# First norm's modulation rows: from split weights on four columns of the array to raw float32 weights on its four column strips

## The reference

```python
silu_c = jax.nn.silu(c)          # (1, 2048)
silu_cc = jax.nn.silu(c_ctx)     # (2048,)
mod = (silu_c @ w_ada[l] + b_ada[l])[:, None, :]       # w_ada[l]: 2048 x 12288
mod_c = silu_cc @ w_ada[l] + b_ada[l]
sh_a, sc_a, gt_a, sh_f, sc_f, gt_f = jnp.split(mod, 6, axis=-1)
h = rms_norm(x, g_attn[l]) * (1.0 + sc_a) + sh_a
hc = rms_norm(xc, g_attn[l]) * (1.0 + csc_a) + csh_a
# then h @ w_in, hc @ w_in (2048 x 4928), four attention mixers, w_out, ffn, second block
```

## Time and profile before

| | |
|---|---|
| median of three runs | 3089.66 us (3085.1 to 3093.73) |
| span of the profiled execution | 3084.6 us, mean granted clock 0.967 |
| PE / DVE / ACT / POOL busy | 2872.8 / 1828.0 / 1222.2 / 254.9 us |
| read from HBM | 572.42 MB, 187 GB/s over the span |
| head stage (before the first win matmul) | 0 to 195.55 us |

### The profile page before, as it was taken

One profiled execution on the slowest core, in us unless ns is written; L12 is line 12 of the kernel. 1 busy time (PEld: TensorE's weight loads), 2 busy tenths in 40 slices (PEclk: granted clock), 3 DMA queues, 4 the chain that ended last, 5 costly groups with the idle time before them and its releaser, 6 DMA issues.

```text
span 3084.6 us, 33987 instructions
## 1 busy us (share of the span) xinstructions
PE 2872.8 (93%) x12623; PEld 2288.0 (74%) x12623; DVE 1828.0 (59%) x2117; ACT 1222.2 (40%) x1561; POOL 254.9 (8%) x233
## 2 busy tenths in 40 slices
PE   3788998988989999999989998899999999999997
PEld 2257776756868888888867887788877888888886
DVE  2888988257655555555565444645455655665555
ACT  4542222234434444444434444444444444444443
POOL 3405233000010000000024000000000000000000
PEclk8899999978999999999999999999999999999998
DMA  8788988201755555555545553255545655555652
GB/s 210 253 268 291 310 292 299 97 14 56 254 179 191 191 185 196 190 191 190 190 142 187 195 196 111 95 193 194 195 162 171 201 182 191 188 191 184 197 190 95
DMA packets 284109, 578.93 MB, mean 188 GB/s; under 512 B 9885, under 2 KB 12610, under 8 KB 281466
## 3 DMA queue, kind: packets, MB, share of 16 engines
q1 hardware_dynamic: 280234, 557.00, 55.0%
q0 software_dynamic: 3792, 20.84, 2.1%
HBM read 572.42 MB, written 5.28 MB: 187 GB/s over the span
## 4 chain that ended last, share of the span: by engine, by line
issue 63%; PE 17%; DVE 12%; DVEq 2%; POOL 2%; ACT 1%; DMA 1%; POOLq 1%; ACTq 0%
DVE proj_ctx L1367 6%; PE bank L327 4%; PE bank L329 4%; PE bank L328 4%; DVE w_lo L323 3%; DVEq L1366 2%; PE bank L553 2%; PE bank L586 1%; ACT probs L660 1%; POOL na_rpb_T L1812 1%; PE bank L1649 1%; PE bank L1650 0%; PE bank L1678 0%; DMA w_raw<-in_w_ada 0%; PE bank L1659 0%
## 5 line engine op out<-in xcount | busy, mean ns | idle before, releaser
L323 DVE TENSOR_TENSOR w_lo<-w_raw,w_hi 128x1024 fp32r<-128x1024 f32 (+2 forms) x928 | 1136.5, 1247 | 748.4 <-ACT w_hi L315 735.9
L315 ACT ACTIVATE w_hi<-w_raw 128x1024 fp32r<-128x1024 f32 (+2 forms) x928 | 964.5, 1054 | 1370.9 <-PE bank L329 1118.8
L327 PE MATMUL bank<-w_hi,xa_hi 128*128 128x512 f32 (+1 forms) x2304 | 907.0, 394 | 35.8 <-DVE w_lo L323 32.9
L329 PE MATMUL bank<-w_hi,xa_lo 128*128 128x512 f32 (+1 forms) x2304 | 899.0, 390 | 0.0
L328 PE MATMUL bank<-w_lo,xa_hi 128*128 128x512 f32 (+1 forms) x2304 | 898.8, 390 | 0.0
L327 PEld LDWEIGHTS bank<-w_hi,xa_hi 128*128 128x128 f32 x2304 | 435.7, 189 | 144.1 <-DVE w_lo L323 32.8
L329 PEld LDWEIGHTS bank<-w_hi,xa_lo 128*128 128x128 f32 x2304 | 435.5, 189 | 90.7
L328 PEld LDWEIGHTS bank<-w_lo,xa_hi 128*128 128x128 f32 x2304 | 435.9, 189 | 87.5
L327 PE MATMUL bank<-w_hi,ffn_act_hi 128*128 128x512 f32 x864 | 338.9, 392 | 7.9 <-DVE w_lo L323 7.9
L328 PE MATMUL bank<-w_lo,ffn_act_hi 128*128 128x512 f32 x864 | 338.3, 392 | 0.0
L329 PE MATMUL bank<-w_hi,ffn_act_lo 128*128 128x512 f32 x864 | 338.0, 391 | 0.0
(11 more groups left out here) (274 smaller groups left out, 1870.0 us busy)
## 6 DMA issues: line engine op xcount, KB each, us to landing
w_raw<-in_w_in SPq DMA_DIRECT2D x116, 1024.0 KB, 5.1
w_raw<-in_w_ada SPq DMA_DIRECT2D x96, 1024.0 KB, 5.2
w_raw<-in_w_up SPq DMA_DIRECT2D x64, 1024.0 KB, 5.2
w_raw<-in_w_down SPq DMA_DIRECT2D x64, 1024.0 KB, 5.1
w_raw<-in_ffn_wg SPq DMA_DIRECT2D x44, 1024.0 KB, 5.2
w_raw<-in_ffn_wu SPq DMA_DIRECT2D x44, 1024.0 KB, 5.2
w_raw<-in_ffn_wd SPq DMA_DIRECT2D x44, 1024.0 KB, 5.1
w_raw<-in_w_out SPq DMA_DIRECT2D x32, 1024.0 KB, 5.1
```

What stands on the lines that cost most here:

```text
L315: act.activation(whi[:, slot, ks, 0:w], raw[:, q, ks, 0:w], ACT.Copy)\
L323: dve.tensor_tensor(wlo[:, slot, ks, 0:w], raw[:, q, ks, 0:w], whi[:, slot, ks, 0:w].bitcast(F32), ALU.subtract).then_inc(sem("lo_made"), 1)
L327: pe.matmul(out, xh, wh, start=first, stop=False)
L329: return pe.matmul(out, xl, wh, start=False, stop=last)
```

## The change

Head-stage units are no longer split. PE multiplies the raw float32 weights with plain float32 matmuls: slice j of a unit goes to partitions 32j to 32j+31 of the bank, with a stationary of 32 columns (16 copies of the silu value for x, 16 for the context). So the four slices of a unit lie on the four column strips of the array. DVE adds the whole bank and the bias, loaded to 32 partitions, in one instruction (`take_sums`); `spread_row` sums the strips with a 128-row stationary that picks one row of each strip. A slot is free again when PE has used it (`ada_used`). The table transfers move from POOL to the head of ACT's queue, the bands from chunk 0 to chunk 3, POOL's store of the bias behind all four `modulate`, and the turning of group 3 from before the first win unit to between the second and the third.

```diff
-U_MIX = 4 * N_ADA_1
+N_LOAD_1 = N_ADA_1
+U_MIX = 0
...
-            wait(sp, "lo_made", 8 * u4 + (2 * q - 6))
+            if isinstance(u4, int) and u4 <= 0:
+                wait(sp, "ada_used", 4 * (u4 + N_LOAD_1) + (q - 3))
+            else:
+                wait(sp, "lo_made", 8 * u4 + (2 * q - 6))
             sp.dma_start(raw[:, q, 0:k, 0:w], src).then_inc(sem(f"landed{q}"), 16)
...
-                sp.dma_start(rows_of(c % 2)[4:5, :], t["b_ada"][:, ada_cols(c)]).then_inc(sem(f"b_loaded{c % 2}"), 16)
+                wait(sp, "ada_rows", c - 1)
+                sp.dma_start(b_rows[0:32, c % 2, :], t["b_ada"][:, ada_cols(c)].to_broadcast([32, NCH]))\
+                    .then_inc(sem(f"b_loaded{c % 2}"), 16)
...
         def _(act):
 
+            with nc.allow_non_contiguous_dma(reason="31 x 28 table, once"):
+                act.wait_ge(sem("memsets"), 2)
+                for h in range(4):
+                    for p in (0, 32):
+                        act.dma_start(narpb[p:p + 31, h * 7:h * 7 + 7], t["na_rpb"][0, h, 4:11, :].rearrange("r m -> m r"))\
+                            .then_inc(sem("na_tables_loaded"), 16)
+            act.dma_start(band[:, :], t["na_band"]).then_inc(sem("na_tables_loaded"), 16)
+            act.dma_start(namask[:, :], t["na_mask"]).then_inc(sem("na_tables_loaded"), 16)
...
-            for c in range(N_ADA_1):
-                hi(act, c, 0)
-                hi(act, c, 1)
-                if c:
-                    copy_rows(c - 1, (c - 1) % 2, 4 * c, 2 + (c - 1) % 2)
-                hi(act, c, 2)
-                hi(act, c, 3)
...
+            for g in range(3):
+                turn_h_act(act, g)
...
+            for v in range(2):
+                m = dve.tensor_copy(c32[:, :, 16 * v:16 * v + 16],
+                                    ps[7][:, 16 * v:16 * v + 16].rearrange("p (k a) -> p k a", a=1)
+                                    .to_broadcast([P, 16, 16]))
...
+            def take_sums(c):
+
+                dve.wait_ge(sem("ada_used"), 4 * c + 4)
+                dve.wait_ge(sem(f"b_loaded{c % 2}"), 8 * (c - c % 2) + 16)
+                wait(dve, "ada_combined", c - 1)
+                dve.tensor_tensor(rows_1[:, c % 2, :], ps[2 + c % 2][:, :], b_rows[:, c % 2, :], ALU.add)\
+                    .then_inc(sem("ada_rows"), 1)
+
             for c in range(N_ADA_1):
-                lo(dve, c, 0)
-                lo(dve, c, 1)
-                lo(dve, c, 2)
                 if c:
                     take(c - 1)
-                lo(dve, c, 3)
+                take_sums(c)
...
+            take(N_ADA_1 - 1)
...
-                if i == 0:
-                    take(N_ADA_1 - 1)
+                if i == 1:
                     turn_h_dve(dve, 3)
...
-            def ada_unit(u4, q, k0, bank):
+            def ada_unit(c, q, bank):
+
+                pe.wait_ge(sem(f"landed{q}"), 16 * c + 16)
                 for j in range(KQ):
...
+                    m = pe.matmul(ps[bank][32 * j:32 * j + 32, :], c32[:, 4 * q + j, :], raw[:, q, j, :],
+                                  start=q == 0, stop=q == 3)
+                m.then_inc(sem("ada_used"), 1)
...
-                    m = pe.matmul(ps[v][:, :], spread[:, v, :], rows_of(c % 2), start=True, stop=True)
+                    m = pe.matmul(ps[spread_bank(c) + v][:, :], pick[:, v:v + 1].to_broadcast([P, P]),
+                                  rows_1[:, c % 2, :], start=True, stop=True)
...
-                if c == 0:
+                if c == 3:
...
             spread_row(N_ADA_1 - 1)
-            turn_h_pe(pe, 3)
-            pe.wait_ge(sem("h_lo"), 16)
...
+                if i == 2:
+                    turn_h_pe(pe, 3)
+                if i < 4:
+                    pe.wait_ge(sem("h_lo"), 4 * i + 4)
```

More of the change, by code:

```diff
@@ L286, in build, with spread_bank @@
         STEPS, STEPS2 = head_steps(), head_steps_2()
+        def spread_bank(c):
+            return 2 if c == N_ADA_1 - 1 else 0
         def load(sp, u4, q, src, k=KQ, w=NCH):
@@ L309, in hi @@
             slot = q % 2 if slot is None else slot
-            act.wait_ge(sem(f"landed{q}"), 16 * u4 + 16)
+            act.wait_ge(sem(f"landed{q}"), 16 * u4 + (16 * N_LOAD_1 + 16))
             for h in range(2):
@@ L1034, in b_piece @@
             def b_piece(c):
[L1036 to L1037 removed]
+                wait(sp, "ada_rows", c - 1)
+                sp.dma_start(b_rows[0:32, c % 2, :], t["b_ada"][:, ada_cols(c)].to_broadcast([32, NCH]))\
+                    .then_inc(sem(f"b_loaded{c % 2}"), 16)
+            sp.wait_ge(sem("memsets"), 4)
             for c in range(N_ADA_1):
                 for q in range(4):
[L1041 removed]
+                    load(sp, c - N_LOAD_1, q, w_ada_v[:, q, :, ada_cols(c)])
                 b_piece(c)
@@ L1117, in _ @@
             m.then_inc(sem("x_squares"), 1)
[L1119 to L1123, removed]
-            for c in range(N_ADA_1):
-                hi(act, c, 0)
-                hi(act, c, 1)
-                if c:
-                    copy_rows(c - 1, (c - 1) % 2, 4 * c, 2 + (c - 1) % 2)
-                hi(act, c, 2)
-                hi(act, c, 3)
-                if c == 0:
[L1133 to L1141, removed]
+            act.wait_ge(sem("na_tables_loaded"), 160)
+            act.activation(bandr[:, :], band[:, :], ACT.Copy)
+            act.activation(narpbr[:, :], narpb[:, :], ACT.Copy).then_inc(sem("na_rpb_hi"), 1)
+            act.wait_ge(sem("x_rstd"), 1)
+            for i in range(4):
+                m = act.activation(xin[:, i, :], xin[:, i, :], ACT.Copy, scale=stat(RSTD + i))
+            m.then_inc(sem("x_scaled"), 1)
+            for g in range(3):
+                turn_h_act(act, g)
             def win_copy(c):
@@ L1357, in multiply @@
                 acc = late_sums(c % 2)
-                dve.wait_ge(sem(f"landed{u % 4}"), 16 * (u // 4) + 16)
+                dve.wait_ge(sem(f"landed{u % 4}"), 16 * (u // 4 + N_LOAD_1) + 16)
                 if k == 0 and c >= N_ADA_1 + 2:
@@ L1805, in _ @@
             pool.dma_start(gvec[:, :], bcast(t["g_attn"], D)).then_inc(sem("g_attn_loaded"), 16)
-            with nc.allow_non_contiguous_dma(reason="31 x 28 table, once"):
-                pool.wait_ge(sem("memsets"), 2)
-                for h in range(4):
-                    for p in (0, 32):
-                        pool.dma_start(narpb[p:p + 31, h * 7:h * 7 + 7], t["na_rpb"][0, h, 4:11, :].rearrange("r m -> m r"))\
-                            .then_inc(sem("na_tables_loaded"), 16)
-            pool.dma_start(band[:, :], t["na_band"]).then_inc(sem("na_tables_loaded"), 16)
-            pool.dma_start(namask[:, :], t["na_mask"]).then_inc(sem("na_tables_loaded"), 16)
             rstd_pool(pool, "x", 4, "_squares")
@@ L1825, in _ @@
             pool.wait_ge(sem("x_scaled"), 1)
-            modulate(0)
+            for q in range(4):
+                modulate(q)
             pool.wait_ge(sem("na_bias_made"), 1)
             pool.dma_start(nab_d, nab_1[:, :, :, :]).then_inc(sem("na_bias_stored"), 16)
-            for q in range(1, 4):
-                modulate(q)
             def norm(x, g, width, n, col):
```

55 lines of the change are left out of this document (19 added, 36 removed).

## The result

| | before | changed |
|---|---|---|
| median | 3089.84 us (four runs) | 3044.06 us (3043.91 to 3046.9, four runs) |
| ratio | | 0.9852, 95% interval 0.984 to 0.9865 |
| span of the profiled execution | 3084.6 us | 3045.1 us |
| first transposition behind the mixer stage | 587.1 us | 547.3 us |

A forecast was written before the change was run, and what follows sets the result against it. Head bound by a 26 us load stall, then DVE's split; now load-bound: 60 + 72 + 4.5, `take(7)` at 144, third `w_lo` at 164.1 instead of 203.92. Span 3084.6 less 39, median 5.1 above: 3051 us, range 3032 to 3088.

The forecast's parts named there:

- The unit on PE (1.9 us): Head stage: a unit's eight matmul records on PE take 1.9 us, hidden behind a load of 3.0 us.
- all four strips together: PE's unit if all four column strips overlap: the time of two records, or 0.95 us.
- Rival 1: Strips do not overlap, so PE bounds the head at 3.45 to 3.7 us a unit: 3082 to 3090 us; chance 0.16.
- Rival 2: Each change of strip on PE exposes its weight load: a unit takes 6.2 us, 3127 us and up; chance 0.07.
- The first eight units (60 us): Head loads: the eighth unit lands at 60 us, slightly earlier than 60.8 because PE rather than DVE frees slots.
- The first chunks share the engines with the same transfers as before, whoever issues them: First head loads: moving the table transfers to another queue changes nothing, so the eighth unit lands at about 60 us.
- rival 3: Tables on ACT's queue land after 60 us, each us late costing one; 0.08 late but a gain, 0.03 beyond 100 us.
- The loads (72 + 4.5 us): Remaining 24 head units at 350 GB/s, 3.0 us each, 72 us, plus 4.5 for bias store and pieces: last lands at 136.5.
- 2 us at half clock: Cost of PE's bands in chunk 3 if the clock is half; at full clock the four slots in flight cover them.
- Behind the last unit: End of the head: PE's unit, `take_sums`, `spread_row`, `take(7)` and semaphore hops bring `take(7)`'s end to 144 us.
- The seam (20.1 us): Head to mixer stage: 20.1 us from `take(7)`'s end to the third win unit's `w_lo` at 164.1, DVE idle some 5.
- Rival 4: The seam eats more, or the mixer stage is bound by something that does not move; ten us lost makes 3061.

The follow-up runs named there:

- experiment 5: Changed kernel with a unit's four slices on one column strip or on two instead of four: 3094.45 us (ratio 1.0038) and 3056.87 us (0.9916).
- experiment 2: Changed kernel with the ten table transfers back on POOL's queue, all else as changed: 3039.07 us, ratio 0.985.
- experiment 1: Changed kernel with only the silu moved ahead of the ten table transfers on ACT: 3076.26 us, ratio 0.9962.
- experiment 6: Changed kernel with group 3 turned before the first win unit again: 3029.4 us (0.9825); repeated, 3038.55 beside 3046.96 for the changed kernel.
- bands spread: Changed kernel with table rows, silu first, group 3 turned before the first win unit, and bands in eights behind units of chunks 2 and 3: 3017.06 us.
- experiment 4: Kernel before the change, weights still split, with only its tables loaded as contiguous rows on POOL's queue: 3057.86 us, ratio 0.9908.

## Why the prediction was right, and where it was not

**The bound and the sum.** A stall of 26 us and then DVE's split held the head, and what is gained there is gained for all: 37.1 us at the third `w_lo` (39.8 forecast), 39.8 at the stage's end, 39.5 in the span, where 39 was forecast. The time itself came out 7 us under the forecast of 3051: the sum took the median to lie 5.1 us above the span, and that of the changed kernel lies 1.0 below. Single terms were off too and made up for each other.

**The unit on PE (1.9 us)** was mis-sized: it is 0.93 in a row, and 1.06 as a row of its own. The step that failed is "the second record of a strip has to wait for the first, and only different strips can overlap". With four, all overlap, the bound that the prediction called "all four strips together". The two strips of experiment 5 do not tell the two readings apart: full overlap gives 3.46 / 2 = 1.73, and the sentence's order gives four record times too (1.75 measured). It changed nothing in the sum, as a unit hides behind 3 us of load either way. Rival 1 is excluded by experiment 5, where it was built: its 3.46 us a unit matches the 3.45 to 3.7 of the rival, but its time came to 3094 in place of 3082 to 3090. Rival 2 is excluded too: a weight load of 0.106 to 0.109 us at full clock is hidden at every change of strip (16 records in 1.92 us, experiment 5), though every one uses all rows. The Trainium skill, "TensorE: Matmul & The Clock Gate", Part 3, has such loads overlap only where the row group differs; here the trace does not agree. Its 2.38 for three column tiles is of the same kind as the 3.7 for four measured here (3.46 / 0.93).

**The first eight units (60 us)**: the eighth is multiplied at 61.89, but not in the way the prediction thought. "The first chunks share the engines with the same transfers as before, whoever issues them" failed. On ACT's queue the single-element transfers took little from the engines, but their issue held ACT for 39.5 us, with the silu behind it. That is rival 3 in another place: it looked at when the tables land (needed by 60, there by 52), not at what stands behind them on ACT. The two sides, a hole of 18 us and a higher rate outside it, cancel to 2 us, and experiment 2 shows the same sum for POOL's queue. That is luck, an accident of sizes: with the silu moved ahead the same transfers cost 29 us more at the stage's end (experiment 1).

**The loads (72 + 4.5 us)**: from 61.89 to 138.50 are 76.6 us for the 24 units, as forecast. Where nothing disturbs, a chunk starts every 12 us (53.91, 65.97, 77.89), the prediction's sign. The rate in the free stretches was higher than 350 (374 and 357 GB/s), and the bands took it back (0.74 from 86 to 98 us). They cost the "2 us at half clock" or somewhat more; the clock was 0.66 there.

**Behind the last unit**: `take(7)` ends at 145.1, 144 was forecast. `modulate` fell from 8.87 to 4.94 us for four, which was not foreseen and had no part in the bound.

**The seam (20.1 us)** took 21.7 (145.1 to 166.83), with 8.3 us of idle DVE in place of 5; experiment 6 prices it at 8 to 9. That the change gives something back there was right. Rival 4, a loss of the gain within the mixer stage, did not come. Its sign was a gain at the first win matmul larger by over 10 us than at the stage's end: it is 48.9 (195.55 to 146.61) against 39.8, 9.1 more, about what the seam costs. With the seam undone (experiment 6, first win matmul at 150.44) it is 45.1 against 47.9. Behind the third `w_lo` nothing of the gain is lost.

**What stays open.** From the stage's end to the end of the program the twelve traces of experiments and change take between 2484.6 and 2498.0 us (before: 2497.5), though no edit touches that part. PE's mean granted clock from 600 to 1000 us lies between 0.92 and 0.97. In the traces where it is 0.92 to 0.94 (before, changed, one strip, two strips, silu first, bands spread) the rest takes 2494.5 us or more, in five of the seven where it is 0.96 or 0.97 2488.7 or less; the other two have 2492.1 and 2495.0. What makes the clock differ there was not tried, nor whether it makes the time. This spread is why gains under some 10 us are read here from the marks of the head and not from the medians.

## What to carry to other kernels

A matrix-vector product in plain float32 need not be split to keep up with its loads: on four column strips a 1 MB unit takes PE a third of what its load takes at full clock (0.93 of 3.0 us), and the engines that made the split are free. Before a transfer is put on a compute engine's queue, ask what its issue costs and what stands behind it there: eight transposing loads of single numbers held ACT for 39.5 and 79.17 us beside other loads, the same numbers as rows for 3.49, with one transposition on PE. If a forecast of a sum comes true, check its terms all the same: here some 15 us that could still be had lay in two effects that had cancelled.

## What the runs showed of the hardware

- Plain float32 matmuls with 32 columns on distinct column strips overlap almost fully: 3.46, 1.75 and 0.93 us for the same eight records on one, two and four strips, each record about 0.59 us long at full clock in all three.
- The issue of eight transfers of 31 x 7 single numbers on ACT's queue took 3.49 us as rows, 39.5 as single elements with a gap in the other loads, 79.17 without. With the DMA engines else idle a single-element issue still took 1.4 to 1.6 us in the changed kernel. On POOL's queue an issue took 2.3 us, but all loads together ran at 242 to 244 GB/s over the first 57 to 60 us, and at 189 from 20 to 35 us, where they ran at 375 with the table as rows.
- POOL's 128x512 product of two tensors took 2.2 us each beside a busy DVE and 1.24 where DVE had little to do (four in 8.85 to 8.89 us in chunks 1 to 3 of the kernels that split, before and experiment 4, in 4.92 to 4.98 in all others). No experiment here isolated it. The Trainium skill, "GPSIMD Engine Reference", Key points, says that GpSimd contends with DVE instructions that have two inputs in SBUF. The trace agrees: `w_lo` is one of that kind, and the changed kernel has none in these chunks but for the ones of the turnings from chunk 5 on.
